# A chunked RWKV scan with its sixteen steps written out, in place of two loops with register waits

## What is computed

```python
def step(S, inp):
    r_t, w_t, k_t, v_t, kk_t, b_t = inp
    sa = -jnp.einsum("bhvk,bhk->bhv", S, kk_t)
    S = S * w_t[:, :, None, :] + sa[..., None] * b_t[:, :, None, :] + v_t[..., None] * k_t[:, :, None, :]
    return S, jnp.einsum("bhvk,bhk->bhv", S, r_t)
...
s_fwd_c, y_fwd_c = rwkv_scan(zero_state, fc, 0, reverse=False)
s_bwd_c, y_bwd_c = rwkv_scan(zero_state, fc, 1, reverse=True)
_, y_fwd_x = rwkv_scan(s_fwd_c, fx, 0, reverse=False)
_, y_bwd_x = rwkv_scan(s_bwd_c, fx, 1, reverse=True)
```

## Time and profile before

| | |
|---|---|
| median of 3 runs | 2407.56 us (2400.04 to 2407.66) |
| profiled execution | 2409.67 us |
| its span, first to last instruction | 2407.5 us |
| scan of layer 0 | about 222 to 517 us of the span |
| scan of layer 1 | about 1600 to 1859 us |
| PE busy over the span | 2071.7 us (86%) |
| DVE, ACT, POOL busy | 1075.5, 774.1, 298.1 us |

### The profile page before, as it was taken

The page is one execution under the profiler, slowest core; times in us unless marked ns, Lnnn a source line. Parts: engine busy times, 40 slices in busy tenths (PEclk is TensorE's granted clock), DMA queues, the critical chain, the costliest instruction groups (busy, mean ns, idle before and its releaser), DMA issues. The chain is left out here.

```text
span 2407.5 us, 51837 instructions
## 1 busy us (share of the span) xinstructions
PE 2071.7 (86%) x22247; PEld 1642.9 (68%) x22247; DVE 1075.5 (45%) x1753; ACT 774.1 (32%) x1419; POOL 298.1 (12%) x380
## 2 busy tenths in 40 slices
PE   4886776777998999889998998968877798988998
PEld 2653676754457888668886675737767456988998
DVE  1644554563282333353332115466645435445544
ACT  1343222223352322142222113253322244434432
POOL 1112222210100001010001001033312020000000
PEclk7997989888998999999999998979989899999999
DMA  7425000030102333212335853100000311553543
GB/s 258 149 85 195 4 4 4 4 109 29 35 2 68 93 104 97 88 53 88 105 105 189 305 167 110 40 1 1 1 4 29 110 36 55 169 174 123 189 162 123
DMA packets 144590, 220.55 MB, mean 92 GB/s; under 512 B 6846, under 2 KB 123800, under 8 KB 137216
## 3 DMA queue, kind: packets, MB, share of 16 engines
q1 hardware_dynamic: 142880, 215.74, 26.4%
q0 software_dynamic: 1504, 1.71, 0.2%
HBM read 208.00 MB, written 9.44 MB: 90 GB/s over the span
## 5 line engine op out<-in xcount | busy, mean ns | idle before, releaser
L366 PE MATMUL BANK<-H_high,W_high 128*128 128x512 f32 (+2 forms) x1472 | 524.7, 356 | 72.1 <-ACT H_high L629 32.3
L330 DVE TENSOR_TENSOR W_low<-RING,W_high 128x1024 fp32r<-128x1024 f32 x268 | 327.8, 1232 | 468.6 <-ACT W_high L327 468.5
L367 PE MATMUL BANK<-H_low,W_high 128*128 128x512 f32 (+2 forms) x1472 | 520.0, 353 | 0.0
L368 PE MATMUL BANK<-H_high,W_low 128*128 128x512 f32 (+2 forms) x1472 | 519.4, 353 | 0.0
L327 ACT ACTIVATE W_high<-RING 128x1024 fp32r<-128x1024 f32 x268 | 279.2, 1052 | 621.3 <-PE BANK L368 592.1
L366 PEld LDWEIGHTS BANK<-H_high,W_high 128*128 128x128 f32 (+1 forms) x1472 | 284.0, 193 | 118.1 <-issue 50.7
L367 PEld LDWEIGHTS BANK<-H_low,W_high 128*128 128x128 f32 (+1 forms) x1472 | 284.2, 193 | 37.9 <-issue 1.1
L368 PEld LDWEIGHTS BANK<-H_high,W_low 128*128 128x128 f32 (+1 forms) x1472 | 283.5, 193 | 37.8
L1234 PE MATMUL BANK<-RING,WORK 64*64 64x64 f32 x4096 | 170.4, 220 | 12.1 <-issue 4.1
L1056 POOL TENSOR_TENSOR WORK<-WORK,masks 128x256 f32<-128x256 f32 x160 | 120.7, 761 | 332.5 <-ACT WORK L1097 226.1
L1234 PEld LDWEIGHTS BANK<-RING,WORK 64*64 64x64 f32 x4096 | 146.8, 135 | 21.8 <-issue 21.2
(11 more groups left out here) (276 smaller groups left out, 3131.4 us busy)
## 6 DMA issues: line engine op xcount, KB each, us to landing
modulation_weights<-w_mod_dram SPq DMA_DIRECT2D x48, 1024.0 KB, 6.6
RING<-w_in_dram SPq DMA_DIRECT2D x46, 1024.0 KB, 5.6
RING<-w_ffn_in_dram SPq DMA_DIRECT2D x44, 1024.0 KB, 5.2
RING<-w_ffn_out_dram SPq DMA_DIRECT2D x20, 1024.0 KB, 5.1
RING<-w_out_dram SPq DMA_DIRECT2D x8, 1024.0 KB, 5.1
h_high<-H_high SPq DMA_DIRECT2D x2, 2048.0 KB, 7.2
h_low<-H_low SPq DMA_DIRECT2D x2, 2048.0 KB, 12.3
H_high<-h_high SPq DMA_DIRECT2D x2, 2048.0 KB, 12.2
```

What stands on the lines that cost most here:

```text
L330: low_ready.mark(nc.vector.tensor_tensor(self.part(1, c), self.raw(c), self.part(0, c).bitcast(FP32), ALU.subtract))
L366: nc.tensor.matmul(out, w[0], x[0], start=start, stop=False)
L367: nc.tensor.matmul(out, w[0], x[1], start=False, stop=False)
L368: return nc.tensor.matmul(out, w[1], x[0], start=False, stop=stop)
```

## The change

The loops are gone. Every engine gets all eight steps of a layer as straight code, with Python integers as step numbers, so every token position and every wait value is a constant. `hold` and its semaphores are removed, with all its calls. Nothing of the arithmetic and nothing in the order of the computing instructions is different.

```diff
-    waits_passed = {e: ctx.enter_context(nc.semaphore(f"waits_passed_{e}")) for e in ("pe", "dve", "pool")}
-
-    def hold(eng, name="pe"):
-        eng.sem_inc(waits_passed[name], 1)
...
         def tokens(eng, d, i):
-            t = chunk_of(d, i)
-            return t if isinstance(i, int) else eng.snap(t, min_val=0, max_val=TOK - CHUNK)
+            return chunk_of(d, i)
 
         def run(eng, step):
-            for first, end, need_y in ((0, N, context_y), (N, STEPS - 1, True)):
-                Signal.trips = end - first
-                with eng.Fori(first, end) as i:
-                    step(i, need_y, True)
-                Signal.trips = 1
-            step(STEPS - 1, True, False)
+            for i in range(STEPS):
+                step(i, context_y or i >= N, i < STEPS - 1)
...
                         for d in range(NDIR):
                             pe.wait_ge(*at_step(s_t[d], i, LEVELS, l))
                             pe.wait_ge(*at_step(s_lm[d], i, NL, l))
-                            hold(pe)
```

More of the change, by code:

```diff
@@ L1044, in operands @@
                     pool.wait_ge(*at_step(s_exp, i, 2, d + 1))
-                    hold(pool, "pool")
                     s_ops[d].mark(nc.gpsimd.tensor_tensor(BK[d][:, :, 1], KD[d][:, :, bass.ds(t, CHUNK)], EXPS[d][:, 2], ALU.mult))
@@ L1137, in exponents @@
                     dve.wait_ge(*at_step(s_exp, i, 2))
-                    hold(dve, "dve")
                     nc.vector.tensor_tensor(EXPO[:, 0], whole, EXCL[1][:, :, at], ALU.subtract)
```

## The result

| | before | after |
|---|---|---|
| median | 2407.12 us (2400.04 to 2407.66, 4 runs) | 2319.68 us (2315.99 to 2321.75, 4 runs) |
| profiled execution | 2409.67 us | 2315.99 us |
| its span | 2407.5 us | 2314.2 us |

The ratio is 0.9642, with an interval of 0.9618 to 0.9665: 87 us faster. The direction was right and the size was less than half of what came.

What follows compares the result with a forecast made beforehand. The prediction took PE's code fetch at branches back to lengthen the scan's steps. Branches -38.2, resident steps lost +7, waits -8 gave -39.2 us: 2370.5 for the profiled execution, 2369 us as median, range 2343 to 2393.

Steps and rivals of the forecast that it cites:

- Part 4: PE's waits and `hold`: 0.06 us saved at each of nine waits a step, 8 us gained, bounds 0 and 16.
- Part 1: PE's seven dear branches back to the body with y become fall-through steps: 38.2 us gained, bounds 27 and 44.
- Parts 2 and 3: PE's straight steps with y pay 2.8 us for code; layer 1's three resident steps without y lose 7 us.
- s = 0.4 us a packet: PE's idle time for each packet of straight code, taken from four fall-through steps at 0.28 to 0.57 us.
- Part 5: Loops of the other engines written out: their extra code is hidden by their slow pace, priced at nothing.
- Straight code is hidden: Rival on PE's code fetch: straight code costs no idle time (s = 0), gain 83 us, 2325 us; chance 0.12.
- A loss I exclude: Within the waits' part: no loss there, since no wait is added and PE's order is the same.
- Dearer: Rival: all steps stream like the worst, s about 0.55, waits bring only 2 us; gain 17 us, 2391; chance 0.24.
- slower: Rival: code streams are the bound, every packet of PE's code stalls it; at s = 1, 2434 us; chance 0.05.
- not the branch: Rival: long steps come from the lower granted clock, not PE's branch; gain under 7 us, about 2403; chance 0.04.

Runs made afterwards that it cites:

- the first experiment: The changed kernel (straight code, constants) with every `hold` put back: 2373.52 us, ratio 0.986 to the kernel before.

## Why the prediction was off, step by step

**Part 4, the waits and `hold`, is the step that failed:** "9 x 0.06 is 0.54 us, x 16 steps, 8.6 us; I take 8", with 0 and 16 us as bounds. Taking `hold` away made the kernel 54 us faster by the whole times and 60 to 65 us by the scans. The latency itself was sized well: behind ACT's copy-out in a level PE's loads are idle for 0.15 us without `hold` and for 0.21 us with it, the 0.06 us of the forecast. What was missed is that a wait placed on the sequencer keeps it from going on. That is shown by the kernel with the increments ahead of the waits. How it makes the steps longer is the reading that fits the rows below: with `hold` nothing behind the wait is taken in until the semaphore comes; with the wait on the matmul, the sequencer takes in the matmuls behind it meanwhile, and PE has a store of work when code comes late. Whether the code is also ordered earlier then, no run tells.

The place just before the last level of one step shows both. In the changed kernel the sequencer passes the mask's wait (L1280) at 303.2 us, when PE has only begun the sixteen loads ahead of that point. PE's load behind it comes 1.5 us later, with DVE named as what ended the wait:

```profile
L1280 PEldq EVENT_SEMAPHORE  x1: 51/51/51, 303.2 to 303.2; - x1
```

```profile
303.23 0.55 PEld L1217 LDWEIGHTS BANK<-RING,WORK 64*64 64x64 f32 x16
...
304.74 0.33 PEld L1239 LDWEIGHTS BANK<-RING,WORK 32*32 32x32 f32 x16 [0.96 <-DVE RING L1172]
```

With `hold` the sequencer's instruction runs at 303.9 us, together with the load, and the idle time is put down to "issue":

```profile
L406 PEldq EVENT_SEMAPHORE  x1: 51/51/51, 303.9 to 303.9; - x1
```

```profile
303.94 0.36 PEld L1252 LDWEIGHTS BANK<-RING,WORK 32*32 32x32 f32 x16 [0.89 <-issue]
```

So "issue" in the kernel before mixed two things, waits of its own for other engines and code that wasn't there. The Trainium skill draws the same difference between the two kinds of wait ("Perfetto Trace Analysis", section "Per-instruction lifecycle: what the profiler-reported window actually captures"): for an instruction of the sequencer the semaphore wait lies in the sequencer, while a matmul goes to a wait queue and the sequencer reads on. The trace agrees, by the 1.5 us above.

What this does to a step is seen in two at the same granted clock, 1.00. Weight loads with idle time ahead of them, in the changed kernel's stretch 400.24 to 428.61 (28.37 us long):

```profile
401.63 0.20 PEld L1230 LDWEIGHTS BANK<-eye_heads,RING 64*64 64x64 f32 x7 [0.62 <-issue]
...
409.22 0.54 PEld L1217 LDWEIGHTS BANK<-RING,WORK 64*64 64x64 f32 x16 [0.39 <-DVE RING L1172]
...
425.58 2.07 PEld L1230 LDWEIGHTS BANK<-WORK 64*64 64x64 f32 x66 [1.24 <-issue]
```

And with `hold`, in the stretch 413.78 to 445.58 (31.80 us):

```profile
415.20 0.30 PEld L1243 LDWEIGHTS BANK<-RING 64*64 64x64 f32 x9 [1.36 <-issue]
...
420.24 0.36 PEld L1243 LDWEIGHTS BANK<-eye_heads,RING 64*64 64x64 f32 x9 [0.56 <-issue]
...
425.52 0.57 PEld L1230 LDWEIGHTS BANK<-RING,WORK 64*64 64x64 f32 x16 [1.23 <-issue]
...
428.94 0.57 PEld L1230 LDWEIGHTS BANK<-RING,WORK 64*64 64x64 f32 x16 [0.36 <-issue]
...
441.73 0.13 PEld L1243 LDWEIGHTS BANK<-WORK 64*64 64x64 f32 x2 [1.29 <-issue]
```

The 3.4 us between the two come apart like this:
- Pauses inside a group of loads that wait for nothing: 1.36 + 0.56 + 1.29, and 1.23 - 0.36 beyond what that place has elsewhere, 4.1 us, against 0.62 + 1.24 = 1.9 us. That is 2.2 us.
- The held waits are slower to end: summed over all rows with idle time in the step, 4.5 us against 4.1. That is 0.4 us, and x 16 it is 7 us, the 8 of the forecast.
- The rest is the loads themselves (22.56 against 22.28 us busy) and gaps too short for the view to print.

At lower granted clocks more is added. Over the fourteen stretches the kernel with `hold` is 451.7 - 391.6 = 60.1 us longer; 337.1 - 313.5 = 23.6 of them are longer PEld time, with a clock of 0.93 on average against 0.97, and 36.5 are idle. That the lower clock follows from the pauses is argued (the instructions that compute are the same), not shown; no run separates the two.

The two totals of these stretches, with `hold` and without:

```profile
sum 451.69, PE 361.75 PEld 337.07 DVE 243.32 ACT 137.75 POOL 121.93; mean PE 25.84 PEld 24.08 DVE 17.38 ACT 9.84 POOL 8.71
```

```profile
sum 391.59, PE 337.60 PEld 313.49 DVE 243.24 ACT 137.69 POOL 121.72; mean PE 24.11 PEld 22.39 DVE 17.37 ACT 9.83 POOL 8.69
```

**Part 1, the branch, was right.** The long steps and the 3.5 us pauses are gone. In the kernel with `hold` and constants the seven steps take 225.1 us in place of 264.6, 39.5 us gained where 38.2 were forecast; with registers it is 34 us. Announcing the branch brought 59 us with everything else left, but that is no check of the 38: there the body also stays in the engine, so that the loop's steps pay for no code at all.

**Parts 2 and 3, straight code, were right only for straight code with `hold`.** With `hold` and constants, the three steps without y lose 7.1 us, as forecast, but the four that fell through before lose another 7.2, so that 39.5 - 7.1 - 7.2 = 25 us are left. With registers the sum is about the same: 34 us gained, and 11 lost by the three. All four steps from which I took s = 0.4 us a packet contained `hold`, the fact that I had beside me and did not weigh: I read s as a price of the packet alone, when it holds for a packet that comes while the sequencer is held again and again.

The idle time of PE's loads in a step with y shows it. In resident steps, with `hold`, it is 3.8 to 4.4 us, which is what the waits take. In fetched steps it is 4.9 to 9.8 us with `hold` (mean 8.2) and 4.3 to 6.9 us without (mean 5.4). So with `hold` late code costs some 8.2 - 4.2 = 4 us a step. Without it, where the profile names the waits, 0.5 to 3.1 us (mean 1.6) are left to "issue". The packets are the same in number, seven or eight a step. Without y it is 6.7 to 7.2 us with `hold` and 4.7 to 4.8 without, all of them waits. My estimate of a resident step with y, 29.5 us, was high too; it measured 27.9.

**Part 5, other engines, was right:** nothing, either way. That the register operations bring nothing by themselves was right too.

**The rivals.** "Straight code is hidden", 2325 us at 0.12, comes within 6 us of the time, but by luck. Its reason, a stream that never turns back, is refuted by the first experiment, and its sum stands on the 29.5 us: with the 27.9 that a resident step takes, twelve such steps give 19 us less, 2306 us. The Trainium skill ("Runtime: NRT & Kernel Launch", section "Instruction fetch mechanics") states that the cost of crossing into the next page is mostly hidden. By the idle times just given, the trace comes nearer to that without `hold` than with it. "A loss I exclude" held. "Dearer", "slower" and "not the branch" are out. The list of what would prove me wrong named steps with y under 30 us and those without under 28, and both came.

What stays open: why PE fetches the body with y again at each branch back in the kernel before, when the announced loop shows that it can stay; the body without y stays without being announced. And how the 40 to 48 us of standing waits divide between missing stock and lower clock.

## What to carry to other kernels

Where a wait sits can be worth more than the latency that it adds: on an engine that runs hundreds of short instructions whose code has to be fetched, keep waits on those instructions and off its sequencer, or the sequencer stands still just when it could go ahead. Where the code stays in the engine, the same waits cost little (27.9 us a step with them). When "issue" ends the idle time of a looped kernel, look first whether a wait is hidden in it, and before taking a price from a stretch, check that the stretch is free of what the change removes. And compare the changed stage by itself as well as the whole time: here a stage that no edit touched moved by 6 us. A loop's branch back that shows records of microseconds can be announced; here that alone brought two thirds of what writing the loop out brought.

## What had not been expected of the hardware

- One announced branch: 0.22 us in place of 3.5 to 4.5, and a body of PE that was fetched anew, with nine packets in the trip shown, stays where it is (109 packets in the run against 172).
- 596 increments of a semaphore cost 9 to 12 us when nothing waits at them (0.015 to 0.02 us each, below the 51 ns of their records), and 54 us when they wait.
- The steps behind a change from one loop body to the next can be as dear as one behind a branch: 31.5 to 37.6 us in the announced kernel.
- With the second wait of a matmul on PE's sequencer, 160 times in the changed kernel, nothing is lost, since each semaphore had been set 0.35 us or more before.
